# Weight loads no longer held back during a triangular inverse, and three panels summed in three equal parts

## The reference, cut to what matters

```
def step(S, inp):
    r_t, d_t, k_t, v_t, kk_t, b_t = inp
    sa = jnp.einsum('bhvk,bhk->bhv', S, kk_t)
    S = S * d_t[:, :, None, :] - sa[..., None] * b_t[:, :, None, :] + v_t[..., None] * k_t[:, :, None, :]
    y = jnp.einsum('bhvk,bhk->bhv', S, r_t)
    return S, y
```

## Time and profile before

| | |
|---|---|
| median of three runs | 1046.74 us (1046.15 to 1050.27) |
| profiled execution | 1047.87 us, span 1046.1 us |
| TensorE busy | 993.2 us, 95% of the span |
| VectorE busy | 752.1 us, 72% |
| ScalarE busy | 525.6 us, 50% |
| loads from HBM | 203.10 MB |
| inverse, from its first product to the last of `TT` level 5 | 145.31 to 207.74 us |
| chunk walk and group norm, to the first product of `wo_a` | 207.74 to 255.09 us |

### The profile page before, as it was taken

The page is one execution under the profiler, slowest core; times in us unless marked ns, Lnnn a source line. Parts: engine busy times, 40 slices in busy tenths (PEclk is TensorE's granted clock), DMA queues, the critical chain, the costliest instruction groups (busy, mean ns, idle before and its releaser), DMA issues.

```text
span 1046.1 us, 19356 instructions
## 1 busy us (share of the span) xinstructions
PE 993.2 (95%) x8274; PEld 864.8 (83%) x8274; DVE 752.1 (72%) x1277; ACT 525.6 (50%) x798; POOL 36.4 (3%) x33
## 2 busy tenths in 40 slices
PE   5999999968999999999999999999999899999996
PEld 4788899967788888788867899999688788999995
DVE  6789889577889958646589665676587895664544
ACT  3358431316454677455366445454466855445442
POOL 0000044200000100000000000000000000000000
PEclk9999999999999999999999999999999999999999
DMA  9674410492456550564264477776646444476411
GB/s 379 248 284 161 162 43 4 162 389 100 154 211 219 221 242 11 232 242 161 81 242 161 170 294 303 287 291 264 240 164 215 188 161 161 172 296 256 171 72 41
DMA packets 15222, 205.40 MB, mean 196 GB/s; under 512 B 1816, under 2 KB 1816, under 8 KB 2976
## 3 DMA queue, kind: packets, MB, share of 16 engines
q1 hardware_dynamic: 14544, 202.55, 50.5%
q10 hardware_dynamic: 592, 1.61, 0.5%
HBM read 203.10 MB, written 1.05 MB: 195 GB/s over the span
## 4 chain that ended last, share of the span: by engine, by line
PE 83%; DVE 10%; ACT 3%; issue 2%; DMA 1%; SPq 0%; DVEq 0%; ACTq 0%
PE bank L455 20%; PE bank L457 20%; PE bank L456 20%; PE bank L758 5%; PE bank L404 4%; DVE slot_parts L2019 2%; PE bank L661 1%; PE bank L562 1%; DMA ring<-in_stream 1%; PE bank L739 1%; PE bank L634 1%; DMA pc<-in_params 1%; PE bank L623 1%; PE bank L900 1%; PE bank L537 1%
## 5 line engine op out<-in xcount | busy, mean ns | idle before, releaser
L455 PE MATMUL bank<-page_parts 128*128 128x512 f32 (+3 forms) x1222 | 428.8, 351 | 6.8 <-DVE page_parts L2301 2.2
L2019 DVE TENSOR_TENSOR slot_parts<-ring,page_parts 128x2048 fp32r<-128x2048 f32 (+2 forms) x117 | 261.4, 2251 | 53.4 <-ACT page_parts L1356 52.9
L457 PE MATMUL bank<-page_parts 128*128 128x512 f32 (+2 forms) x750 | 291.4, 389 | 0.0
L456 PE MATMUL bank<-slot_parts,page_parts 128*128 128x512 f32 (+2 forms) x750 | 290.9, 388 | 0.0
L455 PEld LDWEIGHTS bank<-page_parts 128*128 128x128 f32 x1222 | 232.3, 190 | 36.5 <-issue 3.7
L1356 ACT ACTIVATE page_parts<-ring 128x2048 fp32r<-128x2048 f32 (+2 forms) x121 | 225.0, 1884 | 52.6 <-PE bank L457 28.1
L457 PEld LDWEIGHTS bank<-page_parts 128*128 128x128 f32 x750 | 141.3, 188 | 29.0
L456 PEld LDWEIGHTS bank<-slot_parts,page_parts 128*128 128x128 f32 x750 | 141.8, 189 | 26.8
L1434 ACT ACTIVATE arena<-bank 128x512 f32<-128x512 f32 (+2 forms) x134 | 74.2, 575 | 127.2 <-PE bank L457 67.0
L457 PE MATMUL bank<-page_parts,slot_parts 128*128 128x256 f32 x472 | 133.6, 283 | 0.0
L456 PE MATMUL bank<-page_parts 128*128 128x256 f32 x472 | 133.6, 283 | 0.0
(11 more groups left out here) (318 smaller groups left out, 1114.2 us busy)
## 6 DMA issues: line engine op xcount, KB each, us to landing
ring<-in_stream SPq DMA_DIRECT2D x95, 2048.0 KB, 8.0
arena<-in_x SPq DMA_DIRECT2D x2, 512.0 KB, 4.3
arena<-in_gn ACTq DMA_DIRECT2D x2, 512.0 KB, 4.4
out<-arena SPq DMA_DIRECT2D x2, 512.0 KB, 2.6
cc<-in_consts SPq DMA_DIRECT2D x1, 899.0 KB, 6.6
small<-in_cond ACTq DMA_DIRECT2D x1, 512.0 KB, 10.1
pc<-in_params SPq DMA_DIRECT2D x1, 287.0 KB, 6.8
arena<-in_head_sel ACTq DMA_DIRECT2D x1, 32.0 KB
```

Source lines behind the costliest of these rows:

```text
L455: mm(out, a[0], b[0], start=start, stop=False)
L456: mm(out, a[0], b[1], start=False, stop=False)
L457: return mm(out, a[1], b[0], start=False, stop=stop)
L2019: tt(unit_parts(n)[1], lo, hi, ALU.subtract).then_inc(dv.step("w_lo"), 1)
```

## The change

SP's second wait for `ada_rows` 5 is taken out, so this panel and those behind it are loaded as soon as their slots are free. The 12 quarters of `ada_rows` 5, 6 and 7, which stood as 6 and 6 in the walk, stand as 4, 4 and 4: panel 5 in `beside(4)`, behind level 4 of the inverse; panel 6 ahead of the first new state; panel 7 ahead of the second.

```
@@ block.sync
                     sp.wait_ge(*order[i - SLOTS][1])
-                if name == ("ada_rows", 5):
-                    sp.wait_ge(*finished(("X", 5, 3)))
                 sp.dma_start(ring[:, i % SLOTS, :], stream[i]).then_inc(sem(f"slot_loaded{i % SLOTS}"), 16)
@@ block.vector, beside(l), l == 4
                         tt(GNT[:, tb, :], GNT[:, tb, :], gn[:, 1, :], ALU.add).then_inc(dv.step(), 1)
                     dve.wait_ge(*dv.last)
+                    ada(4)
@@ block.vector, the walk
             for c in range(NC_ - 1):
                 if c < 2:
                     gate_rows(c)
-                    ada(6)
+                    ada(4)
```

## The result

The changed kernel takes 0.28% longer: the ratio of its runs to those of the kernel before is 1.0028, with a 95% interval of 1.0018 to 1.0038, from 20 runs of each (medians 1050.29 and 1047.56 us). In microseconds that is 2.9, between 1.9 and 4.0. The forecast was 4.3. The two profiled executions lie closer than the medians: 1049.35 against 1047.87 us, spans 1047.5 and 1046.1.

A forecast was written before the change was run, and what follows sets the result against it. TensorE carries 83% of the chain and stops for late instruction packets while weights load. The walk begins 7.55 us later and gives back 3.25: 4.3 later, 1051.0 us; range 1045.5 to 1056.5, the forecast case's own 1048 to 1054.5.

The forecast's parts named there:

- What the stops are: TensorE's issue waits: instruction packets of 128 records come late while weights load; a block costs 2.0 to 3.1 us more.
- The inverse, 10.1 us: Products of the inverse: early loads, ada 8 and low clock cost 6.8 + 1.7 + 1.6 us.
- the three stops: Inverse, blocks begun at 147.5, 153.5 and 159.5 us: each loses 2.3 us to a late packet, 6.8 together.
- those behind `ada` 8: Later in the inverse: this panel's load catches one or two blocks, 1.7 us, bounds 0 and 3.1.
- one run at the low clock: Inverse: two bursts, each with half a chance of slow records after it, 1.6 us, bounds 0 and 3.3.
- The walk, 44.1 us: Walk after the inverse: 33.8 + 7.2 + 2.4 + 0.7 us instead of 47.35, giving back 3.25.
- Low-clock runs: Walk: one and a half runs of slow records at the low clock, 2.4 us.
- The extra wait for a state: Walk: without the stops TensorE waits once more for VectorE's new state, 0.7 us.
- The quarters at nothing: Panel 5's four quarters on VectorE end before level 5's first subtraction, so they are free, with 0.9 us to spare.
- Faster: Rival: packets come in time and the inverse loses nothing; 5.8 us less, 1040.9 us; chance 0.08.
- Even: Rival: the walk's loads fall where TensorE waits for a state anyhow; walk 40 us, total 1046.9; chance 0.15.
- Worse: Rival: packets take 6.8 us, the inverse loses 3 x 3.1 + 3.1 + 3.3 = 15.7; 9.9 later, 1056.6 us; chance 0.13.

The follow-up runs named there:

- six loads paced: Changed kernel with ada_rows 5, 6, 7, ada 8, wo_a 0 and 1 loaded in 512 KB pieces, each landing before the next; ratio to kernel before 0.9877.
- pieces of 1 MB: Kernel pacing the same six panels, but in two pieces of 1 MB instead of four of 512 KB; ratio to kernel before 1.0022.

## Why the prediction was right

The forecast said slower by 4.3 us, with slightly better odds for staying within 0.5%; measured is 2.9, within its own range. That 1051.0 us came so close to the measured 1050.29 is partly luck: it started from a median of three runs, 1046.74, which is 1047.56 with twenty, and the change itself is 1.4 us smaller than forecast. The traces show how the parts came out, for one execution of each kernel with 1.4 us between them. Step by step:

- *What the stops are.* That loads beside the products cause them is right, and shown: cutting the loads takes the stops away, doubling them raises the loss of the inverse from 10.1 to 21.9 us (227.25 less 145.46 and 59.9), pacing them removes the stops with all bytes moved. That it is instruction packets that come late is argued, from the distance of 128 records and from the count of q8's packets; no run changed the instructions themselves. The count holds in every kernel: from 145 to 205 us 15, 13, 12 and 10 packets came for 2015, 1709, 1562 and 1326 records (six loads paced, changed kernel, pieces of 1 MB, loads done twice), 130 to 134 records for each.
- *The inverse, 10.1 us.* 2048 records from 145.12 us at the 29.25 ns of the earlier trace rows would end at 205.0; level 5 ended at 215.1, 10.1 later. The parts differ a little: the three stops took 6.0 us (6.8 forecast), those behind `ada` 8 1.3 (1.7), one run at the low clock 1.7 (1.6: 760 records in 23.93 us instead of 22.2). Of the remaining 1.1 us, which I had left out, 0.7 stand behind three of the stops, where 127 or 126 records take 3.94 to 3.98 us, 0.25 more than without a stop. That the sum comes out at 10.1 to the digit is luck: 1.2 too much and 1.2 too little cancel. The stops stand at 151.8, 157.7 and 163.6 us, where 151, 157 and 163 were forecast.
- *The walk, 44.1 us.* This is the step that was mis-sized: 256.52 - 215.15 = 41.4. I let each of the three loads catch one block, 7.2 us; two did, 3.6 us together. Low-clock runs cost more than the 2.4 forecast: 58 records in 3.09 us, 51 in 2.03, 20 in 1.56 and 30 in 1.75 are 3.8 us more than at 29.25 ns each. While the last panel loaded, TensorE was slow and waited for a new state (0.70 at 237.16) anyway, and no stop stands there. The extra wait for a state did not come; there is one, as before. So the walk gave back 6.0 us where 3.25 were forecast.
- *The quarters at nothing.* Right, by the earlier trace rows and the new timeline of VectorE: the last quarter of panel 5 ends ahead of the first subtraction of level 5, which waited for TensorE alone. These are the two rows of the changed kernel:

```profile
210.42 1.22 DVE L1991 CUSTOM_DVE_ANT_0 ring<-ring,small 128x1024 f32<-128x1024 f32 x1
...
212.38 0.69 DVE L2248 TENSOR_TENSOR arena<-arena,bank 128x512 f32<-128x512 f32 x1 [0.74 <-PE bank L758]
```

- *The rivals.* Faster is out: the inverse lost 10.1 us, and that rival needed less than 5.8. Its support was weaker than I made it. The Trainium skill, "DMA: Bandwidth & Descriptors", section "Queues, rings and completion order", lets an engine drain a whole packet, about 9 to 17 descriptors, from one queue before it turns to the next; that a fetch would wait for no more than one row of a panel does not follow from it. No run here shows how much moves in one turn; the pieces of 1 MB against 512 KB show that the wait depends on how much is handed over at once. Even is not what was measured (the interval leaves 1.000 out), though the walk's 41.4 us lie nearer to its 40 than to the 44.1 of the forecast, and its reason, that loads of the walk fall where TensorE waits anyhow, holds for the last panel. Worse is out at this load (10.1 us in the inverse, not 15.7), but the doubled loads show its long stops.

What I did not see at the desk: the kernel before had already paid for these loads, in the walk. Held or not, seven panels came in bursts, and the hold only chose where they hurt. Neither place is needed.

## What to carry to other kernels

Where TensorE runs small products, look for "issue" waits at equal distances in matmul records, with an instruction of TensorE behind each: the engine is then probably out of instructions, and a load of weights that runs at the same time is the likely cause. Do not only move such a load to another time; hand it over in pieces that have landed before the next goes, and check how large a piece the instruction queue tolerates (here 512 KB, not 1 MB). Pacing has a price, the time that each piece takes to land: here 136 GB/s were enough for six panels, and with the seventh the loads became the longest chain.

## What the runs showed of the hardware

- While whole panels are loaded, TensorE stops at equal distances of 128 matmul records (about 256 instructions, 16 KB by the packets of q8): in the inverse for 1.3 to 2.2 us in the changed kernel, for 2.2 to 3.3 us with the loads done twice. With a quiet queue it does not stop once in 52 us, and with pieces of 512 KB not once in 60 (six loads paced) or once for 0.23 us (four).
- The stop does not depend on the length of the rows of a load (4 KB and 16 KB: 1.95 and 1.94 us at the first stop), and not on the mean rate (161 GB/s with and without stops).
- A load takes 3.7 us from issue to landing with 512 KB, 5.2 with 1 MB and 8.2 with 2 MB (medians; the first from the kernel with six paced loads, the second from the one with pieces of 1 MB, the third from both).
- After each stop the next block of 127 records takes about 0.25 us more.
- The granted clock falls with some stops and not with others: it was 1.00 in the 19 us with three stops and 0.93 in the 25 behind them; with six loads paced it is 1.00 in the walk, from 205 to 237 us.
